# Thirty-two row steps leave the sample attention and go to the expert stage

## The reference

```
x = x + W_o [ attention(h) ; pooling(h) ]      h = RMSNorm(x)
x = x + experts(RMSNorm(x))

sample attention, one sequence of 4 tokens against 2048 cached positions in 16 pages:
  k = rms_norm([latent @ w_uk, rope key]);  p = softmax(q k);  o = (p @ latent) @ w_uv

experts, per token: 8 heads pick 16 of 16384 experts each
  a = gelu(u[e] . h)      g = softmax of the picked scores
  y = sum over the 128 picks of g * a * v[e]
```

## Time and profile before

| what | value |
|---|---|
| three runs | 3525.69, 3528.5 (the median), 3542.07 us |
| profiled execution | 3539.48 us |
| its span, first to last instruction | 3537.7 us |
| busy in the span | PE 81%, DVE 77%, POOL 50%, ACT 27% |
| mean traffic | 254 GB/s |
| granted TensorE clock, mean | 0.889 |

### The profile page before, as it was taken

The page is one execution under the profiler, slowest core; times in us unless marked ns, Lnnn a source line. Parts: engine busy times, 40 slices in busy tenths (PEclk is TensorE's granted clock), DMA queues, the critical chain, the costliest instruction groups (busy, mean ns, idle before and its releaser), DMA issues. The chain is left out here.

```text
span 3537.7 us, 40997 instructions
## 1 busy us (share of the span) xinstructions
PE 2876.8 (81%) x12893; PEld 2138.4 (60%) x12893; DVE 2727.1 (77%) x5301; ACT 968.1 (27%) x1627; POOL 1771.3 (50%) x1379
## 2 busy tenths in 40 slices
PE   6655687886698866667737889999999999999996
PEld 3445344665333333357637777778778787787775
DVE  3237688797598847749988868888888888888886
ACT  2211132432133321111106732222222222222221
POOL 0035555366355526626555535566656655555553
PEclk9677898786799988778868999999999999999998
DMA  3321577588799968840003589999999989999987
GB/s 117 110 91 48 186 273 270 168 295 282 245 363 338 336 223 310 320 161 24 30 1 144 239 308 334 336 342 336 336 333 333 350 327 333 340 343 340 335 312 261
DMA packets 311864, 899.73 MB, mean 254 GB/s; under 512 B 34393, under 2 KB 125834, under 8 KB 301386
## 3 DMA queue, kind: packets, MB, share of 16 engines
q0 software_dynamic: 156672, 570.49, 44.7%
q1 hardware_dynamic: 153018, 323.80, 25.1%
q10 hardware_dynamic: 2016, 3.67, 0.3%
HBM read 844.45 MB, written 53.64 MB: 254 GB/s over the span
## 5 line engine op out<-in xcount | busy, mean ns | idle before, releaser
L126 POOL DMA_INDIRECT x_got<-u_rows,x_expert x544 | 730.1, 1342 | 561.2 <-DVE x_got L141 412.6
L126 POOL DMA_INDIRECT x_got<-v,x_expert x544 | 679.8, 1250 | 638.8 <-DVE x_y L148 490.5
L148 DVE SCALAR_TENSOR_TENSOR x_y<-x_got,x_hidden,x_y 128x1024 f32<-128x1024 f32 x544 | 695.3, 1302 | 47.0 <-DMA x_got<-v,x_expert 37.7
L141 DVE SCALAR_TENSOR_TENSOR x_got<-x_got,x_y 128x1024 f32<-128x1024 f32 x544 | 648.4, 1221 | 46.5 <-DMA x_got<-u_rows,x_expert 45.1
L1787 PE MATMUL e_a<-h2h,e_uh 128*128 128x512 f32 x1024 | 407.3, 398 | 57.3 <-DVE e_ul L1867 37.2
L1789 PE MATMUL e_a<-h2h,e_ul 128*128 128x512 f32 x1024 | 401.5, 392 | 0.0
L1788 PE MATMUL e_a<-h2l,e_uh 128*128 128x512 f32 x1024 | 401.3, 392 | 0.0
L1832 ACT ACTIVATE e_vh<-e_v 128x2048 fp32r<-128x2048 f32 x64 | 122.6, 1915 | 568.8 <-PE e_yt L1806 544.4
L820 PE MATMUL d_kn<-w_uk_kept,d_page 128*128 128x512 f32 x512 | 251.4, 635 | 31.3 <-DMA d_krT<-page_krT 27.9
L1787 PEld LDWEIGHTS e_a<-h2h,e_uh 128*128 128x128 f32 x1024 | 193.8, 189 | 118.5 <-issue 60.8
L1789 PEld LDWEIGHTS e_a<-h2h,e_ul 128*128 128x128 f32 x1024 | 193.6, 189 | 41.2
(11 more groups left out here) (402 smaller groups left out, 5576.5 us busy)
## 6 DMA issues: line engine op xcount, KB each, us to landing
e_u<-uT SPq DMA_DIRECT2D x128, 512.0 KB, 6.7
e_v<-v SPq DMA_DIRECT2D x64, 1024.0 KB
gates_d<-g_stage SPq DMA_DIRECT2D x8, 4096.0 KB, 11.3
e_gate<-gates_d SPq DMA_DIRECT2D x32, 1024.0 KB
d_page<-page SPq DMA_DIRECT2D x128, 144.0 KB, 4.5
d_latent<-page_rows SPq DMA_DIRECT2D x128, 128.0 KB
x_got<-u_rows,x_expert POOLq DMA_INDIRECT x544, 6.2
x_got<-v,x_expert POOLq DMA_INDIRECT x544, 6.1
```

Of the source, the lines that this page charges most:

```text
L126: pool.indirect_dma_start(out=self.got[row][:], out_offset=None, in_=self.tables[phase], in_offset=bass.IndirectOffsetOnAxis(ap=self.exper ...
L141: dve.scalar_tensor_tensor(out=row[:], in0=row[:], scalar=1.0, in1=self.y[g][:], op0=ALU.mult, op1=ALU.mult, accum_out=self.hidden[:, g, k ...
L148: dve.scalar_tensor_tensor(out=self.y[g][:], in0=row[:], scalar=self.hidden[:, g, k:k + 1], in1=self.y[g][:], op0=ALU.mult, op1=ALU.add).t ...
```

## The change

```diff
-            sample_attention(nc, a, qk_s, kept, gather, [1, 1, 1, 2] * (PAGES // 4), (0,))
+            sample_attention(nc, a, qk_s, kept, gather, [1] * PAGES, (0,))
```

## The result

The changed kernel takes 3546.46 us in the median, the kernel before 3528.6 beside it (20 runs each). The ratio is 1.0047, with a 95% interval of 1.0035 to 1.006: 16.6 us slower, between 12 and 21. The forecast was +10 us, 3538.5. The profiled execution took 3551.42 us with a span of 3549.6, against 3539.48 and 3537.7 before.

The account below looks back on a forecast made before the run. SP's issuing was taken to pace the sample attention; in the experts PE is busy, held up by DVE's closing steps. Terms -1.4 + 9.3 + 3.5 - 1.3 = +10.1 us on 3528.5 gave 3538.5 us, range 3520 to 3563.

Parts of the forecast that it names:

- SP paces the sample attention: Sample attention: SP's issuing sets the pace, so removing 32 row steps gains only 1.4 us (bounds 0 and -6).
- PE's waits at page 4: Sample attention: a sign to look for, PE's waits for the late key pages growing from 6 to some 10 us.
- The first rival: Sample attention: DVE or the transfers pace it, so most of 44 us is gained, 3496 us; chance 0.08.
- Filled closing slots: Experts, slots 17 and 19 at a round's end: eight filled slots cost their full step, +9.3 us, bound below 0.
- The other 20: Experts, empty slots filled at 2, 5, 8, 11 and 14: covered by DVE's waits, 0 us; 23 us if not.
- Slot 0: Experts, ahead of a round's second `e_ul`: doubled in rounds 0, 8, 16, 24, without slack, +3.5 us (0 to 4.6).
- Openings: Experts: openings of the v steps move from closing slots and slot 0 ahead of the fourth addition, -1.3 us (-3 to +2).
- Traffic 0, bound 6: Experts: 16.8 MB more row fetches, ACT's waits for `e_v` mostly not reaching PE; 0 us, upper bound 6 us.
- The second rival, every step on the path: Experts: DVE bounds the whole round, so all 32 added steps cost time, +35 us, 3563 us; chance 0.12.

## Why the prediction came out as it did

- **SP paces the sample attention: right.** The forecast was -1.4 us; the traces show -1.4 and, with the steps left out, -3.5. That the first agrees to the tenth is luck, since traces of the same phase lie up to 7 us apart; what is shown is that 44 us of DVE's work brought next to nothing. The latents on ACT's queue show the cause: 38 us less in the phase. Wrong in this part was where the freed time would show: DVE waits longer for ACT, and PE's waits at page 4 did not lengthen to 10 us. The first rival failed as its own condition said: SP's issues did not move together when traffic fell. On bytes, the Trainium skill's "Perfetto Trace Analysis", Engine Utilization, by which 333 GB/s is no ceiling, agrees with the 361 GB/s that the same phase reached once SP was relieved.
- **Filled closing slots: right.** +9.3 forecast; +8.4 in the second columns. Of the 1.7 us from the last values to the end, 0.8 lie behind PE's last product, where the forecast had 1.2 for DVE's eighth step. The other 1.0 lie in the products, which ran longer at a lower clock (see the last section) and for which the forecast had no term. Moving the step in all rounds gave 32 to 40 us for 35.
- **The other 20: right.** Filled without the bytes or with them, they leave no new gap of PE at the additions, and DVE's wait for `e_yt` lost 20 us, 23 forecast.
- **Slot 0: right.** +3.5 forecast, +3.2 measured.
- **Openings: wrong.** The step that failed is that the move off the closing slots saves 1.3 us. PE stood 3.89 us ahead of that column before and 4.14 after, as the first two rows show. I had booked 1.4 us for the opening in slot 0 as on the path; the gap behind it was under 0.2 us before, so there was nothing to win there. The third row has a likely reason: behind the 3.89 us PE's clock was at 0.50 in the kernel before, so its column took 2.5 us longer, which is more than that opening. This was not tested.

```profile
2828.76 0.77 PE L1787 MATMUL e_a<-h2h,e_uh 128*128 128x512 f32 x1 [3.89 <-issue]
2875.09 0.51 PE L1787 MATMUL e_a<-h2h,e_uh 128*128 128x512 f32 x1 [4.14 <-DVE e_ul L1867]
2828.00:2834.00 6.00, 5.24 (x12) 4.13 (x13) 5.78 (x7) 1.58 (x2) 2.39 (x1) 0.50 0.88 320
```

- **Traffic 0, bound 6: mis-sized.** PE's gaps ahead of the values grew by 6.6 us in the trace, 2.2 of them in the last round, which varied between 3.6 and 8.4 us over kernels with the same work there. The name of the term is not borne out by the measured times either: without the 32 fetches the time did not fall, though the gaps ahead of the values in rounds 1 to 30 did, to some 7 us. The rows of round 7 show the chain, SP's issue, then ACT and PE:

```profile
2370.73 0.34 SPq L1745 DMA_DIRECT2D e_v<-v  x1
...
2379.23 1.92 ACT L1832 ACTIVATE e_vh<-e_v 128x2048 fp32r<-128x2048 f32 x1 [1.99 <-DMA e_v<-v]
...
2385.95 0.50 PE L1804 MATMUL e_y<-e_wh,e_vh 128*128 128x512 f32 x1 [0.62 <-DVE e_wl L1887]
```

The load is taken up 8.50 us after its issue; in round 7 of the kernel before it was 6.41, with no wait. Over rounds 1 to 31 the mean went from 7.40 to 8.03. Why it grew in rounds that got a closing step is not settled: without the fetch of the added row it was 7.88 us, without DVE's work on it 7.96, and putting the gates behind the values made things worse.

- **The second rival, every step on the path: wrong.** It gave +35, and the runs gave 16.6. It took DVE for the bound of the whole round; the kernel with the moved closing step shows that a step ahead of an addition costs nothing while DVE waits there. The Trainium skill, "Perfetto Trace Analysis", Identifying the Most-Contended Engine, judges PE by its weight loads and not by matmul busy time, and by that DVE was the fullest of the two (86% against 79%); in this case the fullest engine was not what each of the added steps met.

The terms that held sum to -1.4 + 8.4 + 3.2 + 1.7 = +11.9 us in the traces, where the forecast had -1.4 + 9.3 + 3.5 = +11.4. What the forecast lacks is the wait for values, 6.6 of the traces' 18.9 us; with the halved values they give 14.9 - 1.4 = 13.5. By the measured times the halved values take only 1.6 us off the 16.6, with some 6 of uncertainty, so the size of this term stays open.

## What to carry over

A stretch in which three engines look full can still be paced by a fourth that only issues: look at the even spacing of its issues, and at who waits for the last of them. Work taken off an engine there was worth next to nothing until the issuing was relieved, and then the same edit was worth 24 us in that phase. When steps are dealt out to slots, count which slots lie behind the last wait of a round: one step a round moved out of these was worth 32 to 40 us here, more than the 16.6 us that 32 steps moved between phases cost.

## What the runs showed of the hardware

After PE had stood 5.60 us ahead of the last values, its next matmuls took 0.63 us each where they take 0.39 otherwise, and started 0.43 us apart in place of 0.23. PE's timeline of the changed kernel shows it, and below it the windows from 3440 us and over these matmuls:

```profile
3491.15 0.76 PE L1804 MATMUL e_y<-e_wh,e_vh 128*128 128x512 f32 x1 [5.60 <-DVE e_wl L1887]
3491.72 0.63 PE L1805 MATMUL e_y<-e_wl,e_vh 128*128 128x512 f32 x1
3492.14 0.63 PE L1806 MATMUL e_y<-e_wh,e_vl 128*128 128x512 f32 x1
```

```profile
3440.00:3478.00 38.00, 36.40 (x160) 29.51 (x159) 35.19 (x33) 8.30 (x11) 22.77 (x18) 1.00 0.84 300
3491.00:3496.00 5.00, 4.85 (x12) 3.81 (x13) 4.79 (x5) 0.00 (x0) 3.74 (x4) 0.50 0.52 134
```

The granted clock was 0.50 there, the lower of its two levels (1.2 of 2.4 GHz), against 1.00 before the wait. In the sample attention it was 0.93 as long as PE waited 4 to 8 us for pages in each sequence, and 0.98 to 0.99 when SP was relieved. So waits of this length cost PE more than their own time here: ahead of the last values 2.7 us more in the changed kernel, and 1.6 in the kernel before, where PE had stood 3.4 us.
